# Rows spread by transfers, buffers moved and norms on quarter rows in a two-layer decoder step

## The reference

```python
h = rms_norm(x, g_mix) * (1.0 + sc1) + sh1
mix, new_rows = mixer_block(h, pos, past, w_in, w_pa, w_pb, w_out)
x = x + gt1 * mix
h = rms_norm(x, g_ffn) * (1.0 + sc2) + sh2
x = x + gt2 * hier_moe(h, ...)   # 4 groups of 8 experts, 2 experts a token
...
y = rms_norm(x, g_final)
```

## Time and profile before

| | before |
|---|---|
| median of 3 runs | 1081.83 us (1081.15 to 1085.96) |
| profiled execution, its own time | 1082.4 us |
| its span | 1080.6 us |
| TensorE busy | 966.0 us (89%) |
| VectorE, ScalarE, GpSimd busy | 385.9, 294.1, 71.5 us |
| moved by DMA | 318.82 MB, mean 295 GB/s |
| chain that ended last | TensorE 67%, DMA 13%, VectorE 8%, ScalarE 6%, issue 4% |
| mean granted clock of TensorE | 0.971 of full |

### The profile page before, as it was taken

One profiled execution on the slowest core, in us unless ns is written; L12 is line 12 of the kernel. 1 busy time (PEld: TensorE's weight loads), 2 busy tenths in 40 slices (PEclk: granted clock), 3 DMA queues, 4 the chain that ended last, 5 costly groups with the idle time before them and its releaser, 6 DMA issues.

```text
span 1080.6 us, 21869 instructions
## 1 busy us (share of the span) xinstructions
PE 966.0 (89%) x7598; PEld 605.2 (56%) x7599; DVE 385.9 (36%) x1083; ACT 294.1 (27%) x681; POOL 71.5 (7%) x145
## 2 busy tenths in 40 slices
PE   4799999999999997889889999989999899788995
PEld 2467677467864444434456767755786444343443
DVE  2126823223262332223353583132327133222234
ACT  2325565410042111101144455551003211110112
POOL 1012000000100000000001110000010000000000
PEclk9889999999999999989999999999999899999998
DMA  9894322899375999999997333289941399999991
GB/s 374 307 418 171 117 79 95 341 421 411 120 312 213 421 422 422 420 390 410 422 419 237 120 115 118 69 300 421 420 178 40 148 411 422 422 421 419 397 396 44
DMA packets 65420, 318.82 MB, mean 295 GB/s; under 512 B 6050, under 2 KB 27874, under 8 KB 28226
## 3 DMA queue, kind: packets, MB, share of 16 engines
q1 hardware_dynamic: 63408, 314.86, 72.8%
q10 hardware_dynamic: 1810, 2.51, 0.7%
q0 software_dynamic: 128, 0.40, 0.1%
HBM read 315.24 MB, written 2.51 MB: 294 GB/s over the span
## 4 chain that ended last, share of the span: by engine, by line
PE 67%; DMA 13%; DVE 8%; ACT 6%; issue 4%; SPq 1%; POOLq 0%; ACTq 0%; POOL 0%; DVEq 0%; PEldq 0%
PE ps L598 19%; DMA ring<-wstream 13%; PE ps L1098 9%; PE ps L680 7%; PE ps L1075 5%; PE ps L1088 4%; PE ps L1107 4%; PE ps L636 3%; PE ps L1010 3%; PE ps L1078 2%; ACT work L1297 2%; PE ps L746 1%; DVE work L1475 1%; DVE top L1474 1%; ACT L1297 1%
## 5 line engine op out<-in xcount | busy, mean ns | idle before, releaser
L1098 PE MATMUL ps<-ring,h 128*32 128x512 f32 x896 | 113.9, 627 | 25.2 <-DMA ring<-wstream 21.2
L598 PE MATMUL ps<-h,ring 128*128 128x288 f32 x512 | 131.2, 409 | 1.0 <-ACT work L1215 0.9
L598 PE MATMUL ps<-work,ring 128*128 128x288 f32 x512 | 128.7, 409 | 2.4 <-DVE work L1566 2.4
L598 PEld LDWEIGHTS ps<-work,ring 128*128 128x128 f32 x512 | 95.9, 190 | 28.5 <-issue 3.3
L598 PEld LDWEIGHTS ps<-h,ring 128*128 128x128 f32 x512 | 94.9, 190 | 29.1 <-issue 4.4
L680 PE MATMUL ps<-h,ring 128*128 128x288 f32 x416 | 105.0, 413 | 4.3 <-ACT h L1225 2.4
L1361 ACT ACTIVATE mraw<-ps 128x512 f32<-128x512 f32 x64 | 38.2, 597 | 244.8 <-PE ps L1098 244.4
L680 PEld LDWEIGHTS ps<-h,ring 128*128 128x128 f32 x416 | 79.5, 193 | 28.9 <-issue 7.2
L1107 PEld LDWEIGHTS ps<-fold,mraw 128*128 128x128 f32 x512 | 62.0, 191 | 52.0 <-ACT mraw L1361 43.0
L1719 DVE COPY yb<-ps 128x256 f32<-128x256 f32 x64 | 27.2, 425 | 170.0 <-PE ps L1088 170.0
L1107 PE MATMUL ps<-fold,mraw 128*128 128x32 f32 x512 | 68.9, 278 | 20.9 <-PE ps L1088 18.2
(11 more groups left out here) (252 smaller groups left out, 1025.6 us busy)
## 6 DMA issues: line engine op xcount, KB each, us to landing
ring<-wstream SPq DMA_DIRECT2D x272, 1024.0 KB, 15.4
work<-wstream SPq DMA_DIRECT2D x16, 1024.0 KB, 19.0
work<-pages SPq DMA_DIRECT2D x32, 192.0 KB, 3.2
work<-pages SPq DMA_DIRECT2D x32, 128.0 KB, 2.2
x<-x_in SPq DMA_DIRECT2D x1, 1152.0 KB, 5.6
out_y<-h ACTq DMA_DIRECT2D x2, 576.0 KB, 2.8
cs<-consts SPq DMA_DIRECT2D x1, 1026.0 KB, 9.0
out_vp<-work ACTq DMA_DIRECT2D x2, 256.0 KB, 3.2
```

The costliest lines, as they stand in the source:

```text
L598: last = mm(out, w[:, (k0 + k) * stride:(k0 + k) * stride + 128], rhs(k), start=(k == 0), stop=(k == n - 1))
L1098: last = mm(pgu[32 * c:32 * c + 32, :], xs[:, k, :], ws[k // 4][:, c * 512:(c + 1) * 512], start=(k < 4), stop=(k >= 4), skip_group_check= ...
```

## The change: buffers, spreading, waits, norms and loads

The four rows go to partitions 0 to 3 of the dead router weights `sm`; four DMAs of GpSimd's queue spread them (new semaphore `rows_spread`), and `spread_row` and its banks are gone. `sel`, `hit`, `comb` and two of the spread rows now lie in h, the other two in `pads` (the padded queries, zeroed again for the next layer), and `hrow_s` in `yb`. With that the extra slots 3, 4, 5, 6, 7, 2 and 1 are free early: the seventh is loaded once "hs" is made, only the eighth after x7.1.

```diff
-        hrow_s = carve(6912, 256)
-        sel = carve(7168, 3, SLOTS)
+        hrow_s = yb[:, :]
-        extra = [carve(4864 + i * PAIR, PAIR) for i in (3, 4, 5, 6, 7, 2, 0, 1)]
+        extra = [carve(4864 + i * PAIR, PAIR) for i in (3, 4, 5, 6, 7, 2, 1, 0)]
-        drow = hflat[:, 0:4 * T].rearrange("p (i t) -> p i t", t=T)
-        rows4 = hflat[0:4, 7 * T:8 * T]
-        xs = hflat[:, 7 * T:7 * T + KD * BLK].rearrange("p (k s) -> p k s", s=BLK)
-        hit = [hflat[:, (4 + i) * T:(5 + i) * T] for i in range(2)]
-        comb = hflat[:, 6 * T:7 * T]
+        sel = hflat[:, 0:3 * SLOTS].rearrange("p (n s) -> p n s", s=SLOTS)
+        drow = [hflat[:, (6 + i) * T:(7 + i) * T] for i in range(2)] + [pads[:, i * T:(i + 1) * T] for i in range(2)]
+        hit = [hflat[:, i * T:(i + 1) * T] for i in range(2)]
+        comb = hflat[:, 2 * T:3 * T]
+        xs = hflat[:, 3 * T:3 * T + KD * BLK].rearrange("p (k s) -> p k s", s=BLK)
...
@@ SyncE's queue @@
-            sp.dma_start(cs[:, :], consts).then_inc(start_in, 16)
+            sp.dma_start(cs[:, 0:C_SUM], consts[:, 0:C_SUM]).then_inc(start_in, 16)
...
+                    banks.wait_full(sp, of, "hs")
+                    load_extra(of, 6)
                     banks.wait_full(sp, of, f"x{KD - 1}.1")
-                    for j in range(6, EXTRA):
-                        load_extra(of, j)
+                    load_extra(of, 7)
+                if i == KD + 1:
+                    sp.dma_start(cs[:, C_SUM:C_END], consts[:, C_SUM:C_END]).then_inc(consts_in, 16)
@@ GpSimd @@
+                banks.wait_drained(g, l, "rows")
+                for i in range(4):
+                    g.dma_start(drow[i].unsqueeze(1), bc(sm[i:i + 1, l, S_WR:S_WR + T].unsqueeze(1), [1, 128, T])).then_inc(rows_spread, 16)
                 look_ahead(slice(0, 1))
-                far_kept.wait(g, l)
-                for k in range(FAR, KD):
-                    for hf in range(2):
-                        banks.wait_drained(g, l, f"x{k}.{hf}")
+                g.wait_ge(rows_spread, (l + 1) * 16 * 4)
                 hold(g, seen)
                 with g.Fori(0, N_EXP) as e:
                     with g.Fori(0, g.snap(n_blocks, min_val=1, max_val=MAXBLK)) as b:
...
+                        far_kept.wait(g, l)
+                        for k in range(FAR, KD):
+                            banks.wait_drained(g, l, f"x{k}.1")
                         g.wait_ge(gu_done, n + 1)
...
+                if l + 1 < DEPTH:
+                    zp.wait(g, l, 1)
+                    step(padded_again, nc.gpsimd.memset(pads[:, 0:512], 0.0))
@@ TensorE @@
+                            if k == 0:
+                                norm1.wait(pe, l, 5)
...
-                            if hf and k0 == 0 and c % 2:
-                                spread_row(2 * tb + c // 2)
...
-                def up(ws):
+                def up(e, rounds=0):
...
-                        last = mm(pgu[32 * c:32 * c + 32, :], xs[:, k, :], ws[k // 4][:, c * 512:(c + 1) * 512],
+                        if c == 0:
+                            w = expert_weight(e, k // 4, rounds)
+                        last = mm(pgu[32 * c:32 * c + 32, :], xs[:, k, :], w[:, c * 512:(c + 1) * 512],
...
+                def token_sums(m, samples):
+                    for c in range(4):
+                        at, to = c * QT, min((c + 1) * QT, NP)
+                        if samples:
+                            c, at, to = 3, NP, T
+                        last = mm(pgu[32 * c:32 * c + 32, at - c * QT:to - c * QT], ones[:, 0:32], squared[:, m, at:to],
+                                  start=(m == 0 and not samples), stop=(m == KD - 1), skip_group_check=True)
+                        if samples:
+                            break
+                    return last
                 for m in range(KD):
+                    if m == SAMPLES_AT:
+                        sqs.wait(pe, l)
+                        for k in range(KD):
+                            token_sums(k, True)
                     sq.wait(pe, l, KD + m + 1)
-                    mm(pgu[:, 0:NP], ones, squared[:, m, 0:NP], start=(m == 0), stop=(m == KD - 1))
-                sqs.wait(pe, l)
-                for m in range(KD):
-                    last = mm(pgu[:, NP:T], ones, squared[:, m, NP:T], start=(m == 0), stop=(m == KD - 1))
+                    last = token_sums(m, False)
                 ss.up(last)
+                keep_warm(1)
                 if l + 1 < DEPTH:
-                    keep_warm(5)
+                    norm1.wait(pe, l + 1, 2)
+                else:
+                    pe.wait_ge(final, 2)
+                for c in range(4):
+                    last = mm(pgut[:, c * QT:(c + 1) * QT], bc(ident[:, 32 * c:32 * c + 1], [128, 128]), rms[:, 0:QT], start=True, stop=True)
+                last.then_inc(spread_roots, 1)
+                if l + 1 < DEPTH:
+                    keep_warm(2)
@@ ScalarE @@
-                    norm1.wait(a, l, 4)
+                    norm1.wait(a, l, 2)
+                    mods.wait(a, l, 1)
...
+                act(stat[:, 2, 0:1], stat[:, 2, 0:1], ACT.Sqrt).then_inc(sqrt_set, 1)
                 total = a.snap(seen, min_val=1, max_val=200)
...
                 for k in range(KD):
+                    if k == SAMPLES_AT:
+                        xmoe.wait(a, l)
+                        sqs.up(act(squared[:, :, NP:T], x[:, :, NP:T], ACT.Square))
...
-            for k in range(0, KD, 4):
-                a.wait_ge(final, 2 + k + 4)
-                a.dma_start(y_out[:, k:k + 4, :], h[:, k:k + 4, :]).then_inc(y_stored, 16)
+            for k in range(0, KD, 2):
+                a.wait_ge(final, 2 + k + 2)
+                a.dma_start(y_out[:, k:k + 2, :], h[:, k:k + 2, :]).then_inc(y_stored, 16)
@@ VectorE @@
-                for i in range(4):
-                    take(f"bc{i}", drow[:, i, :], banks.ap(l, f"bc{i}")[:, 0:T])
+                d.wait_ge(rows_spread, (l + 1) * 16 * 4)
+                banks.wait_full(d, l, f"x{KD - 1}.1")
```

More of the change, by code:

```diff
@@ L92 @@
 FAR = 4
+QT = T // 4
+SAMPLES_AT = 4
 NEXT_EARLY = 2
@@ L121, in plan @@
         jobs += ["next_t"]
-    jobs += [f"bc{i}" for i in range(4)] + [f"x{k}.1" for k in range(FAR, KD)]
+    jobs += [f"x{k}.1" for k in range(FAR, KD)]
     return jobs
@@ L242, in decoder_trunk @@
         wrow = sb("wrow", [128, 8])
-        qpad_i = sb("qpad_i", [128, NB, 32])
-        qpad = sb("qpad", [128, NB, 32])
+        pads = sb("pads", [128, 2 * T])
+        qpad_i, qpad = (pads[:, i * 256:(i + 1) * 256].rearrange("p (b c) -> p b c", b=NB) for i in range(2))
         stat = sb("stat", [128, 4, GQ])
@@ L324, in decoder_trunk @@
         start_in = sem("start_in")
+        consts_in = sem("consts_in")
         extra_in = sem("extra_in")
@@ L678, in project @@
                         elif c == "qi0":
+                            if k == 0:
+                                norm1.wait(pe, l, 4)
                             normed.wait(pe, l, k // 2 + 1)
@@ L696, in _ @@
                 w = weights(P_QI)
+                if l == 0:
+                    pe.wait_ge(consts_in, 16)
                 project("qi0", w, 0)
@@ L987, in _ @@
                 banks.wait_drained(pe, l, "hs")
-                def spread_row(i):
-                    ps = job(f"bc{i}")
-                    if i == 0:
-                        banks.wait_drained(pe, l, "rows")
-                    filled(mm(ps[:, 0:T], bc(ident[0:4, i:i + 1], [4, 128]), rows4, start=True, stop=True), f"bc{i}")
                 def gather(hf, k0):
@@ L1124, in first_expert @@
                     hold(pe, seen)
-                    ws = [expert_weight(0, i) for i in range(2)]
                     more = look_ahead(next_blocks)
@@ L1139, in expert @@
                 def expert(e, next_blocks, rounds=0):
-                    ws = [expert_weight(e, i, rounds) for i in range(2)]
                     hold(pe, seen)
-                    n = up(ws)
+                    n = up(e, rounds)
                     more = look_ahead(next_blocks)
@@ L1219, in _ @@
                 begin(l, root, exps, rexp, sq, normed, sqs, shift_kept, next_kept, far_kept, shift_rows)
-                square_root(0, rms[:, :])
+                square_root(0, rms[:, 0:QT] if l else rms[:, :])
                 if l == 0:
                     between(["mod0"])
-                    norm1.wait(a, l, 4)
+                    norm1.wait(a, l, 2)
+                    mods.wait(a, l, 1)
                     for k in range(0, KD, 2):
@@ L1227, in _ @@
                     for k in range(KD):
-                        norm1.wait(a, l, 4 + k + 1)
+                        norm1.wait(a, l, 5 + k if k else 3)
                         normed.up(act(h[:, k, 0:NP], h[:, k, 0:NP], ACT.Identity, bias=mod[:, SH1 + k, 0:1]))
@@ L1405, in scales @@
                 def scales():
+                    n = QT if l else T
                     ss.wait(d, l, 0)
```

(18 more changed lines are left out.)

56 lines of the change are left out of this document (32 added, 24 removed).

## The result

The changed kernel takes 1094.72 us (median of 6 runs, 1091.01 to 1095.72) where the kernel before took 1082.92 us beside it (6 runs, 1078.67 to 1085.96). The ratio is 1.0107, 95% interval 1.0078 to 1.0136: slower by 1.1%, where 1.8% faster was forecast. The profiled execution took 1091.6 us, 1089.8 of them span.

The account below looks back on a forecast made before the run. Bounds: the weight stream in each expert stage's first half, TensorE from expert 17, and chains at the seams. Terms 2.7 + 5.2 + 3.0 + 4.3 + 3.3 = 18.5 off 1082.4 give 1063.9, median 1063.3 us; range 1059 to 1091.

Parts of the forecast that it names:

- Spread by four transfers from GpSimd: Before expert 1: four transfers of 0.59 MB in all land by about 333 us, cost zero with 4 us to spare.
- Rival 1: Spread rows, read one after another, land at 349.4 us; expert 1 12.3 us later per layer, 1088 us; chance 0.33.
- rival 2: In between: the spread rows land at 342 to 347 us, total 1076 to 1086 us; chance 0.08.
- Row spreading off TensorE: Inside the second gather: without the spreading products TensorE gains 3.2 us per layer for the first expert.
- Seventh slot early: Extra weight slot loaded into the idle queue before the experts; worth 0, the stream stops earlier at the same gate.
- Half by half: Upward product starts on its first weight half: gains at expert 16 per layer and 31 in layer 0, 2.9 us.
- The norms: Norm at each layer's end: shorter tail and early table load gain 3.0 us between layers, 3.3 at the end.
- rival 3: The early table for the norms doesn't hold and reloads: 2 x 2.6 us come back, 1068.5 us; chance 0.04.
- Start: Kernel start: most constants move behind nine ring slots, so mod0's weights and ScalarE's first scaling come earlier; 2.7 us.

Follow-up runs that it names:

- experiment 1: The run x1_spread_by_tensor: the changed kernel with the four rows spread by TensorE again instead of by transfers; 1066.7 us.
- experiment 5: The run x14_unread_transfers: x1_spread_by_tensor plus the four transfers into scratch memory that nobody reads; 1088.6 us.
- x1_spread_by_tensor: The changed kernel with the four rows spread by TensorE products and VectorE copies again, the rest kept; 1066.7 us, 0.9857 of the kernel before.
- x14_unread_transfers: x1_spread_by_tensor plus the four transfers from partitions 0 to 3 into unread scratch memory, waited for only after layer 0's last expert; 1088.6 us, ratio 1.0062.
- x17_consts_whole: x1_spread_by_tensor with the constants loaded whole at the start (1026 KB), not in two transfers; 1068.6 us, 0.9871 of the kernel before.
- x3_four_ports: The changed kernel with the same four transfers reading partitions 19, 22, 25 and 28 instead of 0 to 3; 1068.6 us, 0.9882 of the kernel before.

## Why the prediction was wrong

**The step that failed** is "Spread by four transfers from GpSimd": "I take 1.4 plus that 3.7: landed by about 333 ... Cost zero, with 4 us to spare." Issue to landing was 22.3 and 22.9 us. The row that it leaned on, a store from 32 partitions in 3.7 us, moves 32 KB a transfer where these move 144, and from many partitions where these four read neighbours. It was no likeness in either. The prediction's own upper bound of 22.4 us, a single engine's rate, was right to 0.1 us in layer 0. In the prediction's terms "cost zero" measured 34.6 us: the 28.0 of experiment 1, and the 6.6 that taking the spreading off TensorE should have gained in two layers.

**Rival 1 had the mechanism of the landing, not the whole price.** It expected the landing at 349.4; it came at 343.3 (321.05 plus 22.26), since the rows themselves were ready 6.6 us sooner (3 by the clock; and the forecast put them at 325.3, the kernel before's time, though its own term for the start brings all forward by 2.7). 343.3 lies in the window that the prediction gave to rival 2, landing at 342 to 347 for 1076 to 1086 us; the total shows that the price of such a landing was too low there too. The total was 6.7 us above its 1088 and above the range's 1091. It charged only the chain from the rows to expert 1. Not in it: the transfers hold the sixteen engines, so extra slot 7 waits; register loads of all engines take 3 to 8 us instead of 0.3 meanwhile; and half clock follows TensorE's pause. By experiment 5 the transfers cost 21.9 us with nothing of the expert stage waiting for them, against 34.6 with it. The difference, some 13 us give or take the scatter of 3, is an estimate of what the wait for the rows adds. The profiles put it lower. From the last product before the experts to expert 1 it is 5.8 and 6.1 us in the two layers of x1_spread_by_tensor, 14.2 and 17.2 in x14_unread_transfers, 19.6 and 20.6 in the changed kernel: 19.5 us lost to the unread transfers, 8.8 more to the wait. Either way it is the smaller part. The two run side by side: in layer 0 of the changed kernel TensorE's own products end only 1.7 us before expert 1.

**Row spreading off TensorE**, 3.2 us a layer: held. From the first product of the second gather to L1055 the changed kernel takes 9.5 us (318.64 to 328.09), x1_spread_by_tensor 12.7 (321.62 to 334.35).

**Seventh slot early**, worth nothing: held (0.8 us, within scatter). Its reason is only half right: the queue of the kernel before isn't dry at 349 us, its DMA share over 342 to 352 us is 0.99.

**Half by half**, 2.9 us: not seen. Undoing it gave 2.9 us slower on one base and 2.7 faster on the other, a scatter as large as the term. The wait for the ring up to expert 16 is 1.33 us between the halves (x1_spread_by_tensor), not the 0.7 expected; where the stream gives one expert every 7.46 us the idle time is what it leaves over, in whatever order TensorE works. Whether the half product ahead pays at expert 16 was not tried further.

**The norms**, 3.0 and 3.3 us: held. From the last combination's update to the next projection it is 9.8 us instead of 12.9. The first and last rows of that stretch in the changed kernel, then in the kernel before:

```profile
552.09 1.27 DVE L1778 SCALAR_TENSOR_TENSOR x<-ps,mod,x 128x256 f32<-128x256 f32 x3 [1.83 <-PE ps L1090]
...
561.89 12.15 PE L699 MATMUL ps<-h,ring 128*128 128x288 f32 x48
```

```profile
546.97 3.23 DVE L1724 SCALAR_TENSOR_TENSOR x<-ps,mod,x 128x256 f32<-128x256 f32 x8 [1.83 <-PE ps L1078]
...
559.83 11.88 PE L680 MATMUL ps<-h,ring 128*128 128x288 f32 x48 [1.93 <-ACT h L1229]
```

At the end the kernel is 13.4 us behind at expert 31 (1067.20 against 1053.81) and 9.2 at the span's end: 4.2 gained. The early table held too, so rival 3 was false.

**Start**, 2.7 us: measured 3.1 (first projection at 34.27 instead of 37.41). Whether it is in the total stays open: x17_consts_whole put it at 1.9 us, inside the scatter.

**The sum without the transfers** would have been 18.5 less 6.6 for the spreading kept on TensorE, 11.9; x1_spread_by_tensor gained 16.0, by its interval 12.7 to 18.2. So the other terms were roughly right in sum, with some luck: the half waits aren't to be seen, and 4.1 us of the gain stand in no term.

**Not foreseen:** a lead at the end of layer 0 is paid back in small part to the pages: the product that waits for them stands 2.20 us in x1_spread_by_tensor and 3.88 in x3_four_ports, where it stood 1.41 in the kernel before without them. And what makes the scatter of 3 us between such kernels is open; one source is in the profiles, a fall of the clock over 60 to 75 us that some have (0.77) and some haven't (1.00).

## What to carry to other kernels

Price a transfer by where the partitions lie that it reads, not by its bytes: 0.59 MB from four neighbouring partitions took 22 us, from four spread ones 10 to 12. Slow packets cost more than their own landing. They hold the engines that also bring weights, and register loads were 3 to 8 us long beside them, so cover for the reader is no cover for the kernel. Where several engines stop at once by "issue", list their lines: instructions that the busy time leaves out can be the ones that take it. If one transfer is to be judged, run it unread beside the old way: that splits the wait from the harm to the others.

## What the runs showed of the hardware that was not expected

- Reads from four neighbouring partitions (0 to 3, and 64 to 67 alike) go at 26 to 31 GB/s, with the sixteen engines shown as 86 to 92% busy with them: packets of 4,608 bytes take 2.6 us in layer 0 and 2.7 in layer 1, against 0.18 and 0.63 us from partitions 19, 22, 25 and 28. It is the same whether they are written to SBUF or to memory.
- While such packets run, register loads from SBUF take 3 to 8 us on TensorE, VectorE, ScalarE and GpSimd, against a median of 0.29 us; only a few that start near the packets' end take about 1 us. The profile shows the engines as idle by "issue" then: TensorE 8.0 to 12.7 us in the changed kernel and x14_unread_transfers. From four spread partitions TensorE's loads take 0.5 us at most; two of GpSimd's, just after its issues, took 2.3 and 3.9 us.
- TensorE's granted clock was 0.53 in the 10 us after such a pause (342 to 352 us), against 0.88 in the same stretch of x1_spread_by_tensor.
